# Log decays summed on VectorE, the router shift on VectorE, halves at the ends of the expert stages, and evener fillings in a two-layer hybrid backbone step

## The reference, cut to what matters

```python
mc, ms = ada_mod(c_ctx, mod_w[l], mod_b[l]), ada_mod(c, mod_w[l], mod_b[l])   # 6 rows of 1024 for each stream
h = rms_norm(x, norm1_g) * (1 + scale) + shift
x = x + gate * mixer(h)                       # h @ w_in, scan or retention or attention, @ w_out
h = rms_norm(x, norm2_g) * (1 + scale2) + shift2
x = x + gate2 * hier_moe(h)                   # group, then 2 of 8 experts in it, for every token
# HGRN, for each head, in chunks, forwards and backwards:
cum = cumsum(logf, axis=time_in_chunk)        # log decays summed within the chunk
scores = sum_k q[t,k] * key[s,k] * exp(cum[t,k] - cum[s,k])        # causal within the chunk
kv     = (key * exp(cum_last - cum)).T @ v    # what a chunk adds to the state
state  = exp(cum_last) * state + kv
out    = scores @ v + (q * exp(cum)) @ state_before
# router: logits = h @ w_router + b;  h = (x/std) * scale' + shift2
#         so logits = (1/std) * x @ (scale' * w) + (shift2 @ w + b)
```

## Time and profile before

| | us |
|---|---|
| median of 3 runs | 1050.4 |
| lowest and highest | 1048.04, 1050.93 |
| the profiled execution | 1042.98 |
| its span, first to last instruction | 1041.2 |
| TensorE busy | 905.2 (87%) |
| VectorE busy | 314.3 (30%) |
| ScalarE busy | 197.3 (19%) |
| moved by DMA | 329.18 MB, 316 GB/s over the span |
| granted TensorE clock, mean | 0.949 of full speed |

### The profile page before, as it was taken

The page is one execution under the profiler, slowest core; times in us unless marked ns, Lnnn a source line. Parts: engine busy times, 40 slices in busy tenths (PEclk is TensorE's granted clock), DMA queues, the critical chain, the costliest instruction groups (busy, mean ns, idle before and its releaser), DMA issues.

```text
span 1041.2 us, 14206 instructions
## 1 busy us (share of the span) xinstructions
PE 905.2 (87%) x5967; PEld 516.2 (50%) x5967; DVE 314.3 (30%) x774; ACT 197.3 (19%) x366; POOL 34.2 (3%) x62
## 2 busy tenths in 40 slices
PE   1799999979699787997699999999996997789963
PEld 0586556664565444564244444444445654455531
DVE  1120235831732111110277814231037221111203
ACT  3111112340211100100340013543002111111102
POOL 3000000111000000000000000001000000000000
PEclk9899999999799999998889999999997998899987
DMA  9999746999597999999943555146835979999995
GB/s 313 401 389 373 284 172 235 409 414 401 191 408 275 421 421 420 421 421 416 394 174 127 191 193 217 41 162 255 348 137 211 377 299 420 422 420 419 421 416 218
DMA packets 74088, 329.18 MB, mean 316 GB/s; under 512 B 5773, under 2 KB 6149, under 8 KB 50213
## 3 DMA queue, kind: packets, MB, share of 16 engines
q1 hardware_dynamic: 69012, 313.44, 76.0%
q0 software_dynamic: 4400, 13.35, 3.5%
q10 hardware_dynamic: 608, 1.44, 0.4%
HBM read 322.11 MB, written 6.09 MB: 315 GB/s over the span
## 4 chain that ended last, share of the span: by engine, by line
PE 70%; DMA 19%; DVE 3%; SPq 3%; ACT 2%; issue 1%; DVEq 0%
PE PS L763 68%; DMA ring<-in_moe_w_gate 11%; DMA ring<-in_mod_w 5%; DMA ring<-in_moe_w_down 4%; SPq L635 1%; SPq L642 1%; SPq L648 1%; ACT scratch L1421 0%; ACT HT L1428 0%; DVE H L1819 0%; DVE X L1814 0%; PE PS L796 0%; DVE scratch L2013 0%; PE PS L1363 0%; PE PS L1093 0%
## 5 line engine op out<-in xcount | busy, mean ns | idle before, releaser
L763 PE MATMUL PS<-ring,scratch 128*32 128x256 f32 (+3 forms) x2592 | 294.5, 461 | 58.8 <-DMA ring<-in_moe_w_gate 39.7
L763 PEld LDWEIGHTS PS<-ring,scratch 128*32 128x32 f32 (+2 forms) x2592 | 140.2, 127 | 205.8 <-issue 158.1
L763 PE MATMUL PS<-ring,HT 128*128 128x512 f32 x432 | 191.9, 598 | 2.7 <-ACT HT L1428 1.9
L763 PEld LDWEIGHTS PS<-ring,HT 128*128 128x128 f32 x432 | 81.2, 191 | 99.2 <-issue 95.5
L763 PE MATMUL PS<-scratch 128*128 128x512 f32 (+3 forms) x480 | 115.9, 427 | 4.6 <-DVE scratch L2477 2.9
L763 PE MATMUL PS<-scratch,H 128*128 128x128 f32 x640 | 84.2, 288 | 3.1 <-DVE scratch L2183 3.1
L763 PEld LDWEIGHTS PS<-scratch 128*128 128x128 f32 (+2 forms) x480 | 56.0, 184 | 59.3 <-issue 51.2
L763 PEld LDWEIGHTS PS<-scratch,H 128*128 128x128 f32 x640 | 79.1, 202 | 10.5 <-issue 10.5
L2296 DVE TENSOR_TENSOR scratch<-PS,scratch 128x256 f32<-128x256 f32 x20 | 8.5, 424 | 188.2 <-ACT scratch L1610 188.2
L763 PE MATMUL PS<-ring,cpad 128*32 128x256 f32 x768 | 48.2, 401 | 18.7 <-DMA ring<-in_mod_w 18.7
L763 PE MATMUL PS<-ring,modrows 128*128 128x512 f32 x120 | 52.5, 592 | 0.0
(11 more groups left out here) (307 smaller groups left out, 707.0 us busy)
## 6 DMA issues: line engine op xcount, KB each, us to landing
ring<-in_moe_w_up SPq DMA_DIRECT2D x64, 1024.0 KB, 18.6
ring<-in_moe_w_gate SPq DMA_DIRECT2D x56, 1024.0 KB, 16.8
ring<-in_moe_w_down SPq DMA_DIRECT2D x56, 1024.0 KB, 16.9
ring<-in_mod_w SPq DMA_DIRECT2D x24, 2048.0 KB, 16.7
ring<-in_odd_w_in SPq DMA_DIRECT2D x12, 2048.0 KB, 12.9
ring<-in_even_w_in SPq DMA_DIRECT2D x7, 2048.0 KB, 16.2
ring<-in_moe_w_down SPq DMA_DIRECT2D x16, 512.0 KB, 17.7
ring<-in_odd_w_out SPq DMA_DIRECT2D x4, 2048.0 KB, 7.6
```

Of the source, the lines that this page charges most:

```text
L763: return nc.tensor.matmul(out, lhsT, rhs, start=start, stop=stop, skip_group_check=True, **kw)
```

## The change

1. Decays: two scans along time (`tensor_tensor_scan`, with a row `WITHIN` of ones that is zero at each chunk's start) replace the 16 transposes, 4 copies and 16 triangle products. VectorE subtracts (`powers`), ScalarE takes the exponentials from SBUF. For group 0 this is done before the fourth projection is read.
2. Fillings: every even input block after the first is followed by one mod block in the stream, and the TensorE order of fillings follows it.
3. Norm 1: x is not scaled; TensorE multiplies x with a diagonal matrix of 1/std (`turn_norm`).
4. Router: `router_shift` multiplies and sums over 8 tiles on VectorE; TensorE sums over the partitions with two products. Transposes and logits are interleaved differently.
5. Expert stages: the second stream's input is multiplied by its gain early (`gain_h`) and finished in one instruction (`finish_h`) in place of two; `ORDER` is written before the first selection matrix; the last scatter, the residual and the second stream's square sums go by halves of 512; six 128-column products stand between the two parts of the last down projection.

```diff
     for i, c in enumerate(EVEN_ORDER):
         items.append(("even_in", c))
-        if i in MOD_BANK:
+        if i:
@@ VectorE, at the fourth projection
+                if c == IA_:
+                    for d in range(2):
+                        lf = LF[:, d, :, :].rearrange("p h t -> p (h t)")
+                        lf = lf[:, ::-1] if d else lf
+                        dve.wait_ge(lf_ready, d + 1)
+                        V.tensor_tensor_scan(lf, WITHIN, lf, 0.0, ALU.mult, ALU.add).then_inc(sums_ready, 1)
+                    powers(0)
+                    products(0)
@@ TensorE, group g
-            turn_decays(0)
-            turn_decays(1)
-            half_chunk()
-            cumulate(0)
...
             for g in range(4):
-                if g == 1:
+                if g < 3:
                     half_chunk()
-                elif g == 2:
-                    late_mod(7)
-                elif g == 3:
+                else:
                     late_mod(5)
...
-                if g < 2:
+                if g < 3:
                     half_chunk()
...
+                pe.wait_ge(masked_ready, g + 1)
+                late_mod(5)
...
-                if g < 3:
-                    cumulate(g + 1)
...
                 group_out(g)
@@ TensorE
-            def logit_shift(l, s, bank):
+            def logit_shift(l, bank):
...
+                matmul(at, cst("ones"), LSHIFT[:, :, :], True, False)
+                matmul(at, cst("ones")[0:1, :], bcast(rbias[:, l:l + 1, :], [1, S, NG + NE]), False, True)\
+                    .then_inc(lshift_done, 1)
+            def turn_norm(s):
+                for k in range(KT):
+                    mm = matmul(PS[:, 2 * s + k // 4, P * (k % 4):P * (k % 4) + P], X[:, s, P * k:P * k + P], DIAG[:, s, :],
+                                True, True)
@@ TensorE, last expert step and end of the stage
+                            if not j:
+                                for _ in range(6):
+                                    matmul(PS[:, 6, 0:P], ident, ident, True, True)
...
-                    scatter((NSTEP - 1) % 2, streams=[s]).then_inc(moe_done, 1)
+                    for half in range(2):
+                        if not s and half:
+                            pe.wait_ge(yg1_ready, NSTEP * (l + 1))
+                        matmul(PS[:, 2 * s + half, :], WSELT[:, (NSTEP - 1) % 2, s, :], YG[:, half, :], False, False)\
+                            .then_inc(moe_done, 1)
@@ VectorE, the decays of a group
+            def powers(g):
+                c, last, mid = decays(g)
+                dve.wait_ge(sums_ready, g % 2 + 1)
+                if g:
+                    dve.wait_ge(decayed_turned, g)
+                V.tensor_tensor(E23[:, :, P:2 * P].rearrange("p h (n t) -> p h n t", t=SUB), last, c, ALU.subtract)\
+                    .then_inc(powers_set, 1)
...
+                V.tensor_tensor(E1[:, :, :].rearrange("p h (n t) -> p h n t", t=SUB), c, mid, ALU.subtract)\
+                    .then_inc(powers_set, 1)
@@ VectorE
+            def diagonal(n, s):
+                dve.wait_ge(rstd_ready, 2 * n + s + 1)
+                V.tensor_scalar(DIAG[:, s, :], ident, rstd[:, s:s + 1], None, ALU.mult).then_inc(diag_ready, 1)
@@ mixer_end
                 shift_h(0)
+                gain_h(n, 1)
                 inverse_std(n + 1, 1)
```

More of the change, by code:

```diff
@@ L243, in backbone, with decays @@
         _evend = _at
+        E = sb("E", [P, 4 * BANK])
         LF = H[:, :, :, :].rearrange("p s k c -> p (s k c)").rearrange("p (d h t) -> p d h t", d=2, h=HA)
-        LFT = [LF[:, g % 2, :, P * (g // 2):P * (g // 2) + P] for g in range(4)]
+        WITHIN = E[:, 0:HA * S * P]
+        def decays(g):
+            s, d = g // 2, g % 2
+            c = LF[:, d, :, P * s:P * s + P].rearrange("p h (n t) -> p h n t", t=SUB)
+            last, mid = (SUB - 1, SUB // 2 - 1) if d == 0 else (0, SUB // 2)
+            return c, c[:, :, :, last:last + 1].broadcast_to([P, HA, NSUB, SUB]), c[:, :, :, mid:mid + 1].broadcast_to([P, HA, NSUB, SUB])
         SG = ST.rearrange("p a n -> p (a n)")[:, 0:1024].rearrange("p (h t) -> p h t", h=HA)
         assert _evend <= 11264
-        E = sb("E", [P, 4 * BANK])
         SHIFT = E[:, :].rearrange("p (s n) -> p s n", s=S)
@@ L1063, in _ @@
             pe.wait_ge(mod_ready, 2 + len(MOD_LATE))
-            for s in range(S):
-                logit_shift(0, s, 5)
             pe.wait_ge(mix_ready, 4)
@@ L1413, in load_sqrt, with square, root @@
                 A_(small[:, 153 + n:154 + n], EPS_COL, SQRT)
+            squared = [0]
+            def square(junk, x, total):
+                squared[0] += 1
+                A_(junk, x, SQUARE, accum_out=total).then_inc(sq_ready, 1)
+            def root(total, bias, s):
+                act.wait_ge(sq_ready, squared[0])
+                A_(sumsq[:, s:s + 1], total, SQRT, scale=1.0 / D, bias=bias).then_inc(std_ready, 1)
             def mean_square(n, s, junk):
@@ L1737, in _ @@
             load_sqrt(4)
-            for s in range(S):
-                mean_square(4, s, squares[:, s, :])
+            mean_square(4, 0, squares[:, 0, :])
+            mean_square_halves(4, squares[:, 1, :])
             act.wait_ge(y_ready, 3)
@@ L1841, in mixer_end @@
                 shift_h(0)
+                gain_h(n, 1)
                 inverse_std(n + 1, 1)
             def moe_end(n):
+                l = n // 2
                 dve.wait_ge(gate_in, 32 * (n + 1))
-                dve.wait_ge(moe_done, 2 * (n // 2) + 1)
-                residual(n, 0)
-                dve.wait_ge(moe_done, 2 * (n // 2) + 2)
-                residual(n, 1, half_way=lambda: inverse_std(n + 1, 0))
-                inverse_std(n + 1, 1)
+                for s in range(S):
+                    g = last_gate(l, s)
+                    for half in range(2):
+                        cols = slice(BANK * half, BANK * half + BANK)
+                        dve.wait_ge(moe_done, 4 * l + 2 * s + half + 1)
+                        st.mark(V.tensor_tensor(g[:, cols], PS[:, 2 * s + half, :], g[:, cols], ALU.mult))
+                    st.wait()
+                    if not s:
+                        V.tensor_tensor(X[:, 0, :], X[:, 0, :], g, ALU.add).then_inc(x_ready, 1)
+                        continue
+                    if not l:
+                        inverse_std(n + 1, 0)
+                        diagonal(n + 1, 0)
+                    for half in range(2):
+                        cols = slice(BANK * half, BANK * half + BANK)
+                        V.tensor_tensor(X[:, 1, cols], X[:, 1, cols], g[:, cols], ALU.add)\
+                            .then_inc(x_ready if half else x_half, 1)
+                if not l:
+                    inverse_std(n + 1, 1)
+                    diagonal(n + 1, 1)
             V.memset(modbias[:, :, :].bitcast(mybir.dt.uint32), 0).then_inc(start_dve, 1)
@@ L1879, in _ @@
                 inverse_std(0, s)
+                diagonal(0, s)
             dve.wait_ge(bias_in, 16 * 12)
@@ L2063, in _ @@
                     late_mod(5)
+            router_shift(0)
             router_weights(0)
-            for s in range(S):
-                keep_shift(0, s, 5)
+            keep_shift(0, 5)
             mixer_end(0, ("even_out", 1))
```

275 lines of the change are left out of this document (143 added, 132 removed).

## The result

| | before | changed |
|---|---|---|
| median of the runs taken together, us | 1049.2 (4 runs) | 1022.0 (4 runs) |
| lowest and highest | 1045.35, 1050.93 | 1020.89, 1022.53 |
| the profiled execution | 1042.98 | 1021.46 |
| its span | 1041.2 | 1019.6 |
| TensorE, VectorE, ScalarE busy | 905.2, 314.3, 197.3 | 898.4, 327.0, 193.8 |

The changed kernel is faster: ratio 0.9744, 95% interval 0.9714 to 0.9775. To see where the 21.6 us between the two spans arose, I cut both traces at the same instructions and subtract.

A forecast was written before the change was run, and what follows sets the result against it. TensorE's list was taken to bound the even and odd stages, DMA most of the expert stages. Terms summed to 21.2 us, making the profiled 1042.98 us 1021.8; taken off the median of 1050.4 they gave 1029.2, range 1021 to 1040.

The forecast's parts named there:

- What bounds the kernel: Even and odd stages bound by TensorE's list, expert stages by DMA from 331 us; earlier gains shift that part whole.
- Decays, 9.5 us: Even stage groups: transposes (1.8 us) and three of four triangle products (7.7) leave TensorE's path; the fourth gives nothing.
- Fillings, 3.4 us: End of the even stage: TensorE's waits for the last mod blocks go, gain 3.4 us, bounds 0 to 3.4.
- Router shift, 3.5 - 0.6: Before the even output projection: 3.5 us of shift products go, two products inside the projection cost about 0.6.
- Routing, 0.8: Both routings: last logits sooner, less the costs of early gain and `ORDER`; 0.4 us gained each, bounds 0 to 3.
- First norm, 0.4: At the start: multiplying by a diagonal takes TensorE longer than transposes; 0.4 us charged, bounds 0 to 1.5.
- the 17 that the forecast gave as a sign: Even stage: the output projection would start about 17 us sooner, at 217 us.
- End of the first expert stage, 1.5: Between scatter and odd projection: halves ready x sooner, longer diagonal products cost; 1.5 us gained, bounds -1 and 4.
- the clock that stays up: Rival, 12%: the 2.4 GHz level holds through the ends of the expert stages, about 5 us more gained, 1024 us.
- End of the kernel, 3.5: After the last scatter: x of stream 0 sooner by halves and a shorter tail; 3.5 us gained, bounds 2.8 and 4.5.
- Scans, at nothing: Before the fourth even projection is read: two scans of 1.2 to 3 us cost nothing, with 9 us free for each.
- rival with late scans: Rival, 4%: scans delay group 0's keys' transpose from 9 us a scan; slower than 1050 above about 19.7 us each.

The follow-up runs named there:

- E9: Changed kernel with 16 transposes and four triangle products of constants put back on TensorE, results unread: 1030.6 us.
- E2: Changed kernel with the roots and stream 0's normalisation moved into the idle time before group 2's states: 1020.1 us.
- E8: Changed kernel with the three last even input blocks ahead of all late mod blocks again, in loads and on TensorE: 1029.0 us.
- E1: Changed kernel with a semaphore of their own for the gain rows, so the first scaling doesn't wait for shift rows: 1016.6 us.
- E10: Changed kernel with layer 0's router shift back on TensorE ahead of the output projection: 1018.8 us.
- E4: Changed kernel with the edits of E1, E2 and E3 together: 1011.1 us.
- E11: Changed kernel with layer 0's router shift back on TensorE and the gain rows' own semaphore: 1019.6 us.
- E3: Changed kernel with ScalarE taking stream 1's softmax exponentials ahead of the evacuation of HGRN's second output: 1018.2 us.
- E5: Changed kernel without the six products in the last expert step: 1023.5 us.
- E7: Changed kernel with whole rows at the ends of the expert stages and without the six products: 1028.3 us.
- E12: Changed kernel with six more scans of 1024 elements on VectorE ahead of the two, results unread: 1027.9 us.

## Why the prediction was right, point by point

- **What bounds the kernel**: right. From the first gather to the last down weights the expert stages took 226.06 and 226.22 us (before 225.57 and 227.12) and shifted whole, and the odd stage is the same to 0.01 us.
- **Decays, 9.5 us**: right in size and place. E9 gives 9.8. That the fourth triangle product gains nothing, since VectorE's list stands ahead of group 3, is shown by the idle of 2.1 us and by E2. What the step left out is the clock behind the idle, 1.6 us (kv 0.7, mod block 0.9).
- **Fillings, 3.4 us**: the waits for loads went, and with the router shift the stretch gained 7.3 where 6.9 were forecast. The bounds, 0 to 3.4, were set against the waits of the kernel before: E8 shows that with the old order the shorter list would have met later loads, so that some 4 us more would have been lost (7.1 by the medians, against 3.4). The decays' edit needs this one.
- **Router shift, 3.5 - 0.6**: both sizes right (3.5 and 0.7), and yet the term was worth nothing. I wrote that the shift's products "hid one thing: the last evacuation of attention". They hid a second: the broadcast of the gate, gain and shift rows, issued at the same point. With 3.6 us less between its issue and its first use it is late. E1 and E10 show this from both sides: with the wait given up (E1, E4), the 3.5 us put back (E10) or both (E11), the first routing takes 16.5 us, and 17.5 to 22.4 in the changed kernel and the eight other experiments. Among these nine the wait goes from 1.48 to 3.12. It is long in E2 and E3 (2.67 and 2.77), whose list ahead of the issue is shorter, but in E8 and E9 too (2.93 and 3.12), whose list is longer: an earlier TensorE does not explain it, and what does stays open.
- **Routing, 0.8**: in the second routing 0.7 came; in the first, 2.3 us were lost for the reason above. The bound of 0 was too narrow, since it looked at the order of the instructions alone and not at the DMA that they wait for.
- **First norm, 0.4**: 0.9 up to the even projection, and 1.6 more up to the groups. The clock of the first 5 us of the projection was 0.50 (43 to 48) where before it was 0.71 (42 to 47). Most of this is this execution's: the twelve experiments begin with the same instructions, and in them the mod block ahead of the groups starts at 107.5 to 110.4 us (median 108.4), in the changed kernel at 109.82, before at 107.33. So about 1.0 of the 2.5 us goes with the change, if the one profiled execution of the kernel before is typical. With the late start and the clock behind group 3's idle, the output projection came 13.5 us sooner and not the 17 that the forecast gave as a sign (its own terms give 16.0).
- **End of the first expert stage, 1.5**: 4.3. I had put the clock that stays up among the rivals, at 12%, because "a wait of a us remains on either side". It stayed up all the same through the last products, the scatter and the odd products; E5 to E7 show that the halves and the six products give 2.5 us each there, and that the rest of the change costs 0.9. The forecast and this rival were not alternatives: both came true.
- **End of the kernel, 3.5**: 5.7. Of this, 4.5 stand before the last output row; another 1.2 come from the output's last transfer, which the sum did not look at. Of the 4.5, 2.4 remain in E7 (13.60), so neither the halves nor the six products gave them: the scatter begins 3.47 us after the last down products there, before 4.29, and from x of stream 0 to the last output row it is 5.55, before 7.13.
- **Scans, at nothing**: right (E12 shows 8.9 us of slack), but for the wrong reason. I counted up to the keys' transposes, while TensorE's first half chunk already waits for a copy that stands behind the scans on the same engine. The rival with late scans would have decided from some 6.7 us a scan (2.2 + 8.9 / 2) and not from 9.
- **The time**: the sum, set against the profiled execution, gave 1021.8, and the profiled execution of the changed kernel took 1021.46. The step that failed is the last one, to take the sum off the median of 1050.4. The kernel before scatters between 1042.7 and 1052.2 over its runs here, mostly at lower mean clocks in the longer ones (in one set 0.946 at 1043.11 and 0.940 at 1052.17), while the changed kernel's four runs stay within 1.6 us. Only one execution of the kernel before was profiled, so in which stage the longer ones lose is not shown. The profiled execution was at the fast end of that spread, so 7 us more than the sum went from the median.

## What to carry to other kernels

When work goes from between the issue of a transfer and its first use, the transfer gets as much later for that use: list what is in flight across the removed work, not only what waits for it. Let no instruction wait on a semaphore that it shares with data which it doesn't read. Price a new idle of TensorE twice, once by its length and once by what may run behind it at half clock, and a kept clock as a gain of the same kind.

## What I had not expected of the hardware

- An idle of 1.61 us in the routing was followed by half clock (0.50 from 254 to 259.2), one of 0.64 at the same place was not (E1, 1.00 from 252 to 254). But E12 had the same idle of 1.61 and full clock behind it (1.00 from 260.2 to 262), so its length alone does not decide. In E5 the last down products took 2.88 us after an idle of 2.78, at the end of the same execution 1.92 after 2.42.
- Six broadcasts of 512 KB issued within 3.2 us beside the stream of weights, at 411 GB/s in all (221 to 246 us): the first four took 13 us to land by their median, the second of the shift 24.5. A semaphore over all of them gives the time of the last.
